# Wide matmuls for the u blocks of a gated mixer, with the addition on VectorE, the scaling on GpSimd, and two projections read in the other order

## What is computed

```
z = h @ w_in
za, zb, zg = jnp.split(z, [2 * A_WIDTH, 2 * A_WIDTH + 3 * B_WIDTH], axis=-1)
u, v = jnp.split(jax.nn.gelu(za), 2, axis=-1)
y_a = spatial_gating(u, v, sgu_norm, sgu_w, sgu_b) @ w_proj_a
gate_b, gate_c, xb = jnp.split(zb, 3, axis=-1)
y_b = (gate_b * short_conv(gate_c * xb, conv_w)) @ w_proj_b
g_a, g_b = jnp.split(zg, 2, axis=-1)
merged = jax.nn.sigmoid(g_a) * y_a + jax.nn.sigmoid(g_b) * y_b
return merged @ w_out
```

## Time and profile before

| what | us |
|---|---|
| median of 3 runs | 1060.01 |
| lowest and highest run | 1059.90, 1060.06 |
| the profiled execution | 1060.34 |
| its span | 1058.5 |
| TensorE busy in it | 1048.3 (99%) |
| VectorE busy | 773.9 (73%) |
| ScalarE busy | 614.1 (58%) |
| GpSimd busy | 193.0 (18%) |

### The profile page before, as it was taken

How to read it: one execution, slowest core, us unless ns; L and a number is a source line. 1 busy time by engine, 2 the same in 40 slices (tenths; PEclk the granted TensorE clock), 3 DMA queues, 4 the chain that set the end, 5 groups by cost and what they waited for, 6 DMA issues and landing times.

```text
span 1058.5 us, 17547 instructions
## 1 busy us (share of the span) xinstructions
PE 1048.3 (99%) x6112; PEld 920.2 (87%) x6112; DVE 773.9 (73%) x1107; ACT 614.1 (58%) x936; POOL 193.0 (18%) x208
## 2 busy tenths in 40 slices
PE   8999999999999999999999999999999999999997
PEld 6888888888888888888888888889988888888886
DVE  6876776799797666668767666788877778877543
ACT  7655545466765654447565445755655556655542
POOL 4211131020221111101111100133201032311100
PEclk9999999999999999999999999999999999999999
DMA  7855555554266565566555564656555555655552
GB/s 276 290 192 198 190 188 183 175 180 161 98 210 207 190 190 186 191 196 200 198 189 191 180 206 151 224 182 193 176 195 182 185 179 192 224 196 197 176 188 75
DMA packets 55570, 200.53 MB, mean 189 GB/s; under 512 B 6304, under 2 KB 6304, under 8 KB 55392
## 3 DMA queue, kind: packets, MB, share of 16 engines
q1 hardware_dynamic: 54288, 195.85, 56.0%
q0 software_dynamic: 656, 3.18, 0.8%
q10 hardware_dynamic: 576, 0.83, 0.3%
HBM read 198.78 MB, written 1.05 MB: 189 GB/s over the span
## 4 chain that ended last, share of the span: by engine, by line
PE 97%; ACT 1%; DMA 1%; DVE 1%; issue 0%; ACTq 0%; DVEq 0%
PE pair L1396 52%; PE pair L1397 26%; PE pair L1390 6%; PE pair L1391 5%; PE pair L1392 5%; DMA x<-x_in 1%; PE pair L1743 0%; PE pair L1676 0%; PE pair L1663 0%; PE pair L1607 0%; PE pair L1654 0%; PE pair L1464 0%; ACT qk_a L698 0%; ACT x_hl L486 0%; DVE qk_a L1178 0%; PE pair L1640 0%
## 5 line engine op out<-in xcount | busy, mean ns | idle before, releaser
L867 DVE TENSOR_TENSOR w_lo<-w_raw,w_hi 128x1024 fp32r<-128x1024 f32 x369 | 461.6, 1255 | 213.5 <-ACT w_hi L479 212.8
L1396 PE MATMUL pair<-x_hl,w_hi 128*128 128x512 f32 x1728 | 591.5, 390 | 2.6 <-DVE x_hl L873 2.4
L479 ACT ACTIVATE w_hi<-w_raw 128x1024 fp32r<-128x1024 f32 x369 | 386.1, 1057 | 229.9 <-PE pair L1397 181.4
L1397 PE MATMUL pair<-x_hl,w_lo 128*128 128x256 f32 x1728 | 477.8, 277 | 0.0
L1396 PEld LDWEIGHTS pair<-x_hl,w_hi 128*128 128x128 f32 x1728 | 324.4, 188 | 71.0 <-issue 3.2
L1397 PEld LDWEIGHTS pair<-x_hl,w_lo 128*128 128x128 f32 x1728 | 324.3, 188 | 0.1
L1396 PE MATMUL pair<-wide,w_hi 128*128 128x512 f32 x720 | 247.2, 391 | 0.0
L1397 PE MATMUL pair<-wide,w_lo 128*128 128x256 f32 x720 | 199.6, 277 | 0.0
L1396 PEld LDWEIGHTS pair<-wide,w_hi 128*128 128x128 f32 x720 | 135.2, 188 | 28.8
L390 POOL TENSOR_TENSOR wide<-side,wide 128x256 fp32r<-128x256 f32 x88 | 86.6, 984 | 377.4 <-ACT wide L537 377.4
L1397 PEld LDWEIGHTS pair<-wide,w_lo 128*128 128x128 f32 x720 | 135.1, 188 | 0.0
(11 more groups left out here) (199 smaller groups left out, 860.5 us busy)
## 6 DMA issues: line engine op xcount, KB each, us to landing
w_raw<-stream SPq DMA_DIRECT2D x369, 512.0 KB, 3.3
const<-const_in POOLq DMA_DIRECT2D x1, 1248.0 KB, 8.3
w_raw<-stream SPq DMA_DIRECT2D x4, 256.0 KB, 5.6
rows<-rows_in POOLq DMA_DIRECT2D x1, 576.0 KB, 10.2
x<-x_in ACTq DMA_DIRECT2D x2, 256.0 KB, 5.6
x<-x_in SPq DMA_DIRECT2D x2, 256.0 KB, 6.6
sgu_w<-sgu_w_in POOLq DMA_DIRECT2D x1, 512.0 KB, 12.9
qk_a<-gain_in POOLq DMA_DIRECT2D x1, 512.0 KB, 4.0
```

Of the source, the lines that this page charges most:

```text
L479: nc.scalar.activation(w_hi[:, slot, at:at + BW], w_raw[:, slot, :], ACT.Copy).then_inc(w_hi_done, 1)
L867: nc.vector.tensor_tensor(w_lo[:, slot, :], w_raw[:, slot, :], w_hi[:, slot, at:at + BW].bitcast(F32), ALU.subtract).then_inc(w_split, 1)
L1396: nc.tensor.matmul(dst, a_hi, b_hl.rearrange("p a s -> p (a s)"), start=first, stop=False, skip_group_check=True)
L1397: return nc.tensor.matmul(dst[:, 0:S], a_lo, b_hl[:, 0, :], start=False, stop=last, skip_group_check=True)
```

## The change

The u blocks are computed by `wide_block`. Their bank then holds two parts. ScalarE copies the part 256:512 to `low_s` (new, `u_low`), VectorE adds the two into `u_s` (`u_add`, in place of `u_scale`), and GpSimd multiplies by `rstd` (new, `u_scale`), before Gelu as before. TensorE's waits for free banks change from `u_scaled` to `u_added`. The projection of ya is moved behind that of yb in each group of four, with its weights; the two keep their banks. `feature_block` is no longer there.

```diff
+            def u_scale(m):
+                pool.wait_ge(u_added, m + 1)
+                nc.gpsimd.tensor_tensor(u_s[:, m, :], u_s[:, m, :], rstd[:], ALU.mult).then_inc(u_scaled, 1)
...
             scale_gate_b(KC - 1)
+            u_scale(0)
             conv_lo(KC - 1)
...
-                split(n0 + 36)
-                conv_hi(KC - 1)
...
+                def u_part(m):
+                    act.wait_ge(w_used, n0 + 32 + m + 1)
+                    if m == 0:
+                        act.wait_ge(cx_added, KC)
+                    elif m >= 2:
+                        act.wait_ge(u_added, m - 1)
+                    nc.scalar.activation(low_s[:, m % 2, :], bank[4 + (m + 3) % 4][:, S:2 * S], ACT.Copy).then_inc(u_low, 1)
+                    split(n0 + 36 + m)
+                    if m == 0:
+                        conv_hi(KC - 1)
                     act.wait_ge(u_scaled, m + 1)
                     nc.scalar.activation(u_s[:, m, :], u_s[:, m, :], ACT.Gelu_apprx_tanh).then_inc(u_gelu, 1)
...
-                def u_scale(m):
-                    dve.wait_ge(w_used, n0 + 32 + m + 1)
-                    nc.vector.tensor_tensor(u_s[:, m, :], bank[4 + (m + 3) % 4][:, 0:S], rstd[:], ALU.mult).then_inc(u_scaled, 1)
+                def u_add(m):
+                    dve.wait_ge(u_low, m + 1)
+                    nc.vector.tensor_tensor(u_s[:, m, :], bank[4 + (m + 3) % 4][:, 0:S], low_s[:, m % 2, :],
+                                            ALU.add).then_inc(u_added, 1)
...
-                u_scale(0)
+                u_add(0)
+                conv_output(KC - 1)
                 split(n0 + 36)
-                conv_output(KC - 1)
...
-                    feature_block(n0 + 32 + m, bank[4 + (m + 3) % 4][:, 0:S], x_hi, x_lo)
+                    wide_block(n0 + 32 + m, bank[4 + (m + 3) % 4], x_hl)
...
-                        pe.wait_ge(ya_split, KC)
-                        wide_block(b + 2, bank[4 * j + 2], ya_hl, i, 8)
                         pe.wait_ge(yb_split, KC)
-                        wide_block(b + 3, bank[4 * j + 3], yb_hl, i, 8)
+                        wide_block(b + 2, bank[4 * j + 3], yb_hl, i, 8)
+                        pe.wait_ge(ya_split, KC)
+                        wide_block(b + 3, bank[4 * j + 2], ya_hl, i, 8)
```

More of the change, by code:

```diff
@@ L305, in build @@
         yb_split = sem("yb_split")
+        u_low = sem("u_low")
+        u_added = sem("u_added")
         u_scaled = sem("u_scaled")
@@ L451, in _, with ya_product @@
                     conv_lo(m - 1)
-            scale_gate_b(KC - 1)
-            conv_lo(KC - 1)
-            for m in range(KC):
+            def u_scale(m):
+                pool.wait_ge(u_added, m + 1)
+                nc.gpsimd.tensor_tensor(u_s[:, m, :], u_s[:, m, :], rstd[:], ALU.mult).then_inc(u_scaled, 1)
+            def ya_product(m):
                 pool.wait_ge(u_gelu, m + 1)
@@ L458, in _ @@
                 nc.gpsimd.tensor_tensor(u_s[:, m, :], u_s[:, m, :], sg[:, m, :], ALU.mult).then_inc(ya_done, 1)
+            scale_gate_b(KC - 1)
+            u_scale(0)
+            conv_lo(KC - 1)
+            for m in range(1, 4):
+                u_scale(m)
+            ya_product(0)
+            ya_product(1)
+            u_scale(4)
+            ya_product(2)
+            ya_product(3)
+            for m in range(5, KC):
+                u_scale(m)
+                ya_product(m - 1)
+            ya_product(KC - 1)
             for m in range(KC):
@@ L787, in ya_part @@
                     nc.scalar.activation(ya_hi[:, m, :], u_s[:, m, :], ACT.Copy).then_inc(ya_hi_done, 1)
-                for m in range(3):
-                    u_act(m)
-                    split(n0 + 37 + m)
-                u_act(3)
+                for m in range(4):
+                    u_part(m)
                 ya_part(0)
                 ya_part(1)
-                split(n0 + 40)
-                u_act(4)
+                u_part(4)
                 ya_part(2)
                 ya_part(3)
-                split(n0 + 41)
-                u_act(5)
-                ya_part(4)
-                split(n0 + 42)
-                u_act(6)
-                ya_part(5)
-                split(n0 + 43)
-                u_act(7)
-                ya_part(6)
-                ya_part(7)
+                for m in range(5, KC):
+                    u_part(m)
+                    ya_part(m - 1)
+                ya_part(KC - 1)
                 for m in range(KC):
@@ L1313, in gated_mixer @@
                 ya_part(3)
-                u_scale(6)
+                u_add(6)
+                split(n0 + 42)
                 ya_part(4)
-                split(n0 + 42)
+                u_add(7)
                 ya_part(5)
-                u_scale(7)
+                split(n0 + 43)
                 ya_part(6)
-                split(n0 + 43)
                 ya_part(7)
@@ L1405, in wide_block @@
                     last = both(dst[:], w_hi[:, slot, w], w_lo[:, slot, w], b_hl[:, k, :, :], k == 0, k == KC - 1)
-                last.then_inc(w_used, 1)
-            def feature_block(n, dst, b_hi, b_lo, i=0, per=0, p=None, ready=None):
-                slot = n % RING
-                pe.wait_ge(w_split, n + 1 + per * i)
-                for k in range(KC):
-                    if p is not None:
-                        pe.wait_ge(x_split, 8 * p + k + 1)
-                    if ready is not None:
-                        pe.wait_ge(ready, k + 1)
-                    w = slice(k * P, (k + 1) * P)
-                    last = three(dst, w_hi[:, slot, w], w_lo[:, slot, w], b_hi[:, k, :], b_lo[:, k, :], k == 0, k == KC - 1)
                 last.then_inc(w_used, 1)
@@ L1746, in gated_mixer @@
                 for m in range(4, KC):
-                    pe.wait_ge(u_scaled, m - 3)
-                    feature_block(n0 + 32 + m, bank[4 + (m + 3) % 4][:, 0:S], x_hi, x_lo)
+                    pe.wait_ge(u_added, m - 3)
+                    wide_block(n0 + 32 + m, bank[4 + (m + 3) % 4], x_hl)
                 pe.wait_ge(sg_done, KC)
@@ L1753, in gated_mixer @@
                         if j == 1:
-                            pe.wait_ge(u_scaled, KC)
+                            pe.wait_ge(u_added, KC)
                         wide_block(b, bank[4 * j], x_hl, i, 8)
                         wide_block(b + 1, bank[4 * j + 1], x_hl, i, 8)
+                        pe.wait_ge(yb_split, KC)
+                        wide_block(b + 2, bank[4 * j + 3], yb_hl, i, 8)
                         pe.wait_ge(ya_split, KC)
-                        wide_block(b + 2, bank[4 * j + 2], ya_hl, i, 8)
-                        pe.wait_ge(yb_split, KC)
-                        wide_block(b + 3, bank[4 * j + 3], yb_hl, i, 8)
+                        wide_block(b + 3, bank[4 * j + 2], ya_hl, i, 8)
                 base = 4 + PAIRS
@@ L1889 @@
         np.stack([z[c + m] for m in range(KC) for c in (24, 32, 16)]), z[0:8],
-        np.stack([b[m] for m in range(KC) for b in (z[40:48], z[48:56], pa, pb)]),
+        np.stack([b[m] for m in range(KC) for b in (z[40:48], z[48:56], pb, pa)]),
         _features(w1["w_out_2"]),
```

7 lines of the change are left out of this document (3 added, 4 removed).

## The result

The changed kernel takes 1061.76 us (median of 22 runs, 1059.48 to 1069.32), the kernel before in the same comparison 1060.00 (22 runs, 1059.76 to 1060.50). The ratio is 1.0023, 95% interval 1.0014 to 1.0032: slower by 1.8 us, and spread over 10 us where the kernel before keeps within 0.8. The forecast was 1059.1, 0.9 us faster; the time lies inside the range that was stated with it, 1057.6 to 1063.4. The profiled execution took 1063.12 us, of which the span is 1061.3.

A forecast was written before the change was run, and what follows sets the result against it. TensorE was taken as the bound, busy 1048.3 of 1058.5 us. Fourth block +2.4 (u-block gains included), fast pace -3.3, so -0.9: 1060.34 - 0.9 = 1059.4, less 0.33 to the median, 1059.1; range 1057.6 to 1063.4.

The forecast's parts named there:

- The u blocks: On TensorE, 64 pairs replace 64 triples; a gain of 0.85 us was taken.
- one floor a triple: Estimate from the Trainium skill's matmul formula: a triple saves one 2.5 ns floor against a pair, 0.16 us in all.
- The chain: Steps producing ya on ScalarE, VectorE and GpSimd: a slice stretches to 3.69 us, as GpSimd and VectorE exclude each other.
- The standstill: TensorE waits 3.4 us for ya ahead of the fourth wide block, plus 0.1 for the first pair.
- The fall of the clock: TensorE's clock falls during its wait for ya, giving 1060.9 (fast pace) or 1064.2 us (slow); chance 0.05.
- rival 4: The clock falls while TensorE waits for ya, costing 1.8 us as in the warm-up; chance 0.05.
- The pace behind the standstill: 41 blocks from the fourth to 881.0: fast pace takes 3.3 us less, slow changes nothing; weighed about even.
- The sign: Whole kernel: -0.9 us at the fast pace, +2.4 at the slow; within 0.2% 0.58, slower 0.30, faster 0.12.
- the walk: Step-by-step timing of four engines through the region, putting the end of ya's last subtraction at 768.4 us.
- rival 2: TensorE waits for ya and the blocks behind run at the slow pace: 1062.4 us, 1061.7 to 1063.2; chance 0.35.
- the triples hand it on: The slow pace at 757.80 came out of the u blocks' back-to-back triples, costing 3.5 us over 44 blocks.
- the reset by a plain float32 matmul: U blocks 4 to 7, behind the plain float32 spatial matmuls, would run fast: -0.51 us, or -0.19 if not.

The follow-up runs named there:

- e1: The changed kernel with the scaling by rstd done on VectorE behind its addition instead of on GpSimd: 1056.61 us, ratio 0.9969.
- e7: The changed kernel with VectorE's rests of weight blocks n0+36 to n0+43 and of ya replaced by a multiplication with 0.5: 1056.3 us, ratio 0.9965.
- e5: The changed kernel with 14 unused plain float32 matmuls on TensorE ahead of its first wait for ya: two groups, 1058.98 to 1059.34 and 1061.92 to 1062.54 us.
- e14: The changed kernel again, unedited, for another trace: median 1066.09 us over 4 runs, traced run 1063.00.
- e12: The kernel with the scaling on VectorE, plus 24 matmuls in triples, both operands from x_hl, ahead of the gates and projections loop: 1059.76 us.
- e16: The kernel with the scaling on VectorE, plus 96 matmuls in triples, both operands from x_hl, ahead of the gates and projections loop: 1067.7 us.
- e17: The kernel with the scaling on VectorE, plus 24 matmuls in triples using weights of block n0+40, ahead of the gates and projections loop: 1059.42 us.
- e3: The kernel before, with one plain float32 matmul of 128 columns ahead of the gates and projections loop: 1060.27 us, ratio 1.0002.
- e8: The kernel before, with one plain float32 matmul of 256 columns ahead of the gates and projections loop: 1060.45 us, ratio 1.0003.
- e2: The changed kernel with 28 unused plain float32 matmuls on TensorE ahead of its first wait for ya: 1062.13 us, ratio 1.0019.
- e6: The changed kernel with the old order of projections, ya third and yb fourth: 1065.26 us, ratio 1.0051.
- e10: The kernel with the scaling on VectorE, plus nine fills on GpSimd ahead of its last product of u: 1058.54 us, ratio 0.9993.
- e9: The kernel before, with six fills of an unused tile on GpSimd ahead of its last product of u: 1057.25 us, ratio 0.9973.

## Why the prediction was wrong

- **The u blocks:** right. 0.85 forecast, 0.83 found, and spatial matmuls of unchanged length in between. The 0.16 us for one floor a triple, the estimate beside it, is a fifth of that, and it is the pair that saves one, having a matmul fewer.
- **The chain:** right in mechanism and size. A slice of 3.69 us was walked, 3.67 and 3.68 stand in the trace; a product of 1.73, measured 1.72. e1 and e7 bear the cause out. The prediction excepted only operations with an operand in PSUM; the theory of e7 went further and excepted those with one SBUF operand, and was refuted for the operation tried.
- **The standstill:** right. 3.4 + 0.1 forecast, 3.19 found ahead of the same block.
- **The fall of the clock:** this is the step that failed: the sum charged the standstill its own length and 0.1 us for the restart, and nothing for the clock. The fall was rival 4, with a chance of 0.05 and a price of 1.8 us from the warm-up. It came in three of four traces and cost 2.96. The trace of before had no standstill of that size, and the chance was put down as if that spoke against it. The price was taken from the warm-up, 5.19 - 3.4 = 1.8; here what takes 3.06 took 5.92. One trace was little to take it from: the same 16 matmuls took 5.02 us in e5 and 6.57 in the changed kernel, 1.6 to 3.2 us over the 3.4. (That they ran at the lower level is worked out from their pace; the clock in the profile's windows is 1.00 there.) With the standstill of 3.2 for 3.5 the fourth block is +2.1 late, and the case of a fallen clock and the fast pace gives 1060.0 + 2.1 - 3.3 + 2.9 = 1061.7, beside a median of 1061.76. That it meets the median so closely is partly luck, since 11 of these 22 runs have a clock of 0.998 or more and so no full fall. The section "What's actually happening" of the Trainium skill's page TensorE: Matmul & The Clock Gate, named with rival 4, says that an idle TensorE falls back to 1.2 GHz. Three traces of this kernel agree; in e14, with the same standstill, it did not fall.
- **The pace behind the standstill:** right that it is one of two and is worth 3.3 us, and that it can go either way (fast in three traces, slow in e14). The forecast took the two as cases of which one would hold for all runs. They change from run to run, as e14 shows and the two groups of e5 suggest, so that a median need not lie in either case alone.
- **The sign:** the forecast had the gain and the loss nearly equal, 0.58 for "within 0.2%" and 0.30 for slower. The measured 1.8 us, 0.17%, is within that band in size, but the interval does not touch 1. With the clock as likely as the traces make it, three in four, the likeliest time would have been near 1062. That 1061.76 lies inside the range is no merit of the walk: rival 2 had put the upper part of the range there for another reason.
- **What was said of the pace's origin,** that the triples hand it on, is not borne out by e12, e16 and e17, and the reset by a plain float32 matmul is refuted by e3 and e8. What brings it in the kernel before stays open.

## What to carry to other kernels

When an edit lengthens a chain to an engine that never waited so far, price the wait as its length plus what the restart brings: here 0 or 3 us for the clock and 0 or 3 us for the pace, changing from run to run. A spread that appears with a change can be a sign of such a wait: here it went with it in e1 and e2. And count the operations of GpSimd and VectorE together where both read SBUF: the multiplication that cost 0.74 us on GpSimd cost the chain a microsecond more there, and on VectorE (0.42 us) made the change worth 3.5 us instead of -1.8.

## What the runs showed of the hardware

- The granted clock fell to 0.5, the level of 1.2 GHz, behind a standstill of 3.2 us for about 6 us in three of four traces, and behind one of 5.8 us (e6). It stayed at 1.00 in e14 (3.2 us), e10 (1.2 us) and e9 (0.05 us).
- Wide blocks keep 0.340 or 0.350 us a pair, the slow one over 44 blocks in the kernel before. It changed behind a restart 0.05 us late (e9) and behind pairs 0.07 us longer than the others, with no idle time shown (e10). This decides 3.5 us of 1060.
- A plain float32 matmul of 128 columns is two records of 0.110 us, 0.22 us in all.
- A multiplication of 128 x 1024 by a constant took VectorE 0.84 us (e7), a subtraction of two such operands in the same place 1.38; GpSimd's product beside them took 1.18 and 1.72 us instead of 0.74.
